# All of w_out for the two full tiles in split single-pass products, its first halves made during the dense stage, and two expert units prefetched later

## The reference

```
proj  = x @ w_in + b_in                      # 1024 -> 7168: xa ga b c v m_a m_b
h     = rglru(conv4(xa))                     # gates, recurrence over positions
mixed = (sigmoid(m_a) * h * gelu(ga) + sigmoid(m_b) * b * conv3(c * v)) @ w_out   # 1024 x 1024
x     = layernorm(ALPHA * x + mixed)
gates = softmax(top4(x @ router_w + router_b))              # of 32 experts
x     = layernorm(ALPHA * x + sum_e gate_e * ((up + 1) * gate * sigmoid(1.702 gate)) @ w_down[e])
```

## Time and profile before

| | us |
|---|---|
| runs shown, median (lowest, highest) | 1194.64 (1194.02, 1195.10) |
| profiled execution, its own time | 1193.83 |
| its span, from first to last record | 1192.1 |
| PE busy in the span | 1144.1 (96%) |
| DVE busy | 520.6 (44%) |
| ACT busy | 260.0 (22%) |
| DMA: bytes moved, mean rate | 443.78 MB, 372 GB/s |
| granted TensorE clock, mean | 0.994 of full speed |

### The profile page before, as it was taken

The page is one execution under the profiler, slowest core; times in us unless marked ns, Lnnn a source line. Parts: engine busy times, 40 slices in busy tenths (PEclk is TensorE's granted clock), DMA queues, the critical chain, the costliest instruction groups (busy, mean ns, idle before and its releaser), DMA issues.

```text
span 1192.1 us, 13955 instructions
## 1 busy us (share of the span) xinstructions
PE 1144.1 (96%) x5682; PEld 555.9 (47%) x5682; DVE 520.6 (44%) x989; ACT 260.0 (22%) x405; POOL 3.3 (0%) x13
## 2 busy tenths in 40 slices
PE   9999999999999999999999989999999999999994
PEld 8999999663333333333333323333333333333331
DVE  6788788883333333333333332333333333333336
ACT  4655655411111111111111111111111111111112
POOL 1000000000000000000000000000000000000000
PEclk9999999999999999999999999999999999999998
DMA  9866964768999999999999999999999999999994
GB/s 231 263 207 174 265 194 130 290 280 347 384 428 426 427 428 428 428 426 428 428 427 428 427 428 427 428 426 428 429 427 427 426 429 428 426 429 427 427 425 161
DMA packets 93853, 443.78 MB, mean 372 GB/s; under 512 B 7912, under 2 KB 65400, under 8 KB 68062
## 3 DMA queue, kind: packets, MB, share of 16 engines
q1 hardware_dynamic: 93614, 442.41, 92.1%
q10 hardware_dynamic: 176, 0.48, 0.1%
HBM read 441.34 MB, written 1.53 MB: 372 GB/s over the span
## 4 chain that ended last, share of the span: by engine, by line
PE 65%; DMA 24%; DVE 7%; ACT 2%; issue 2%; SPq 0%; DVEq 0%; POOL 0%; ACTq 0%; POOLq 0%
PE PS L949 25%; DMA ring<-in_w_gu 19%; PE PS L990 13%; PE PS L737 8%; PE PS L854 6%; DMA ring<-in_w_down 4%; PE PS L876 3%; PE PS L758 2%; DVE w_lo L1096 2%; PE PS L862 1%; DVE tiles L1139 1%; PE PS L869 1%; PE PS L913 1%; PE PS L768 1%; PE PS L1030 1%
## 5 line engine op out<-in xcount | busy, mean ns | idle before, releaser
L949 PE MATMUL PS<-ring,mid 128*64 128x512 f32 x1920 | 422.0, 593 | 20.4 <-DMA ring<-in_w_gu 19.8
L949 PEld LDWEIGHTS PS<-ring,mid 128*64 128x64 f32 x1920 | 135.8, 137 | 299.8 <-issue 258.5
L990 PE MATMUL PS<-ring,mid 128*64 128x512 f32 x952 | 211.3, 595 | 0.0
L1421 DVE TENSOR_SCALAR PS<-PS 128x512 f32<-128x512 f32 x30 | 21.0, 700 | 353.1 <-PE PS L949 353.1
L737 PE MATMUL PS<-x_hi,w_hi 128*128 128x320 f32 x448 | 140.5, 314 | 1.9 <-ACT tiles L555 1.1
L737 PE MATMUL PS<-x_lo,w_hi 128*128 128x320 f32 x448 | 138.4, 309 | 0.0
L737 PE MATMUL PS<-x_hi,w_lo 128*128 128x320 f32 x448 | 138.4, 309 | 0.0
L1403 DVE TENSOR_TENSOR ys<-PS,ys 64x512 fp32r<-64x512 f32 x64 | 44.1, 689 | 193.9 <-ACT ys L642 185.6
L990 PEld LDWEIGHTS PS<-ring,mid 128*64 128x64 f32 x952 | 65.6, 137 | 129.5 <-issue 129.5
L1139 DVE SCALAR_TENSOR_TENSOR x_tok<-PS,gate,x_tok 128x1024 f32<-128x1024 f32 (+1 forms) x93 | 115.2, 1276 | 20.9 <-PE PS L876 20.9
L633 ACT ACTIVATE mid<-PS 128x512 f32<-128x512 f32 x30 | 17.9, 597 | 418.8 <-DVE PS L1421 418.8
(11 more groups left out here) (243 smaller groups left out, 756.2 us busy)
## 6 DMA issues: line engine op xcount, KB each, us to landing
ring<-in_w_gu SPq DMA_DIRECT2D x124, 2048.0 KB, 41.7
ring<-in_w_down SPq DMA_DIRECT2D x59, 2048.0 KB, 40.3
raw<-in_w_in SPq DMA_DIRECT2D x56, 512.0 KB, 5.8
ring<-in_w_down SPq DMA_DIRECT2D x9, 1024.0 KB, 11.9
ring<-in_w_gu SPq DMA_DIRECT2D x8, 1024.0 KB, 7.5
ring<-in_w_out SPq DMA_DIRECT2D x4, 1024.0 KB, 5.0
x_tok<-in_x_prompt SPq DMA_DIRECT2D x2, 512.0 KB, 4.9
x_tok<-in_w_down SPq DMA_DIRECT2D x1, 1024.0 KB, 12.3
```

The costliest lines, as they stand in the source:

```text
L949: last = mm(PS[64 * a:64 * a + 64, b, :], xgT[:, 2 * (u % 2) + j, u // 2, :], w[2 * j + b][:, a * HALF:(a + 1) * HALF], start=False, stop= ...
L990: last = mm(PS[64 * a:64 * a + 64, XB, :], hT[:, j, u, :], w[j][:, a * HALF:(a + 1) * HALF], start=(u == 0 and j == 0), stop=(u == 1 and j ...
L1421: dve.tensor_scalar(gm, gm, LIMIT, None, ALU.min).then_inc(gm_ok, 1)
```

## The change

`HALVED` falls from (0, 1, 2, 4, 10) to (0, 1, 4): units 2 and 10 are whole. `EARLY = {4: 2, 5: 3, 6: 0, 7: 1}` names which chunk of w_out is split in which chunk of the dense stage. `out_hi` now lies in slot 10, `out_lo` in slot 1, so that both exist before the dense stage ends; `out2_hi`, `out2_lo`, `mix2_hi` and `mix2_lo` (slots 9, 8, 7 and in place of `mixT`) hold the parts for chunks 4 to 7. `project` serves tile 2 alone.

```
@@ SP, dense loads
-                    if k < 6:
-                        load_half(k // 2, k % 2).then_inc(unit_in[k // 2], 16)
-                    elif k < KC:
-                        load_out(k - 6)
-                    else:
-                        load_half(10, k - KC).then_inc(unit_in[10], 16)
+                    if k < 4:
+                        load_half(k // 2, k % 2).then_inc(unit_in[k // 2], 16)
+                    elif k == 4:
+                        load_out(1)
+                    elif k == 6:
                         sp.wait_ge(bias_ok, 1)
+                        load_out(0)
@@ SP, after proj_done NP
             load_unit(6)
-            load_unit(9)
+            load_unit(3)
+            sp.wait_ge(first_read, 1)
+            sp.wait_ge(outlo_ok, 2 * HALF_K)
+            load_half(4, 1).then_inc(unit_in[4], 16)
+            load_half(FREED, 0).then_inc(freed_in, 16)
             sp.wait_ge(block_ok, KC + 1)
             load_unit(5)
             sp.wait_ge(first_free, 1)
-            load_unit(3)
-            load_half(4, 1).then_inc(unit_in[4], 16)
-            load_half(FREED, 0).then_inc(freed_in, 16)
+            load_unit(2)
+            load_unit(10)
             sp.wait_ge(wout_done, 5)
             load_unit(8)
+            load_unit(9)
@@ ACT, in the dense loop, before the wait for proj_done
+                if j == 3 and c in EARLY:
+                    k = EARLY[c]
+                    act.wait_ge(wout_in[k // 2], 16)
+                    act.activation(out_hi[:, k, :], out_rows(k // 2)[:, k % 2, :], ACT.Copy).then_inc(outhi_ok, 1)
+                if j == 4 and c == KC - 1:
+                    act.wait_ge(wcur_ok, KC)
+                    act.wait_ge(block_ok, HALF_K + 1)
+                    for t in range(2):
+                        act.activation(mix_s[:, t, 0], mix_of(t), ACT.Copy).then_inc(mixhi_ok, 1)
@@ ACT, after it (the copies of L582 and L586 are gone)
+            for k in range(HALF_K):
+                act.wait_ge(wout_in[2 + k // 2], 16)
+                act.activation(out2_hi[:, k, :], out_rows(2 + k // 2)[:, k % 2, :], ACT.Copy).then_inc(out2hi_ok, 1)
+            act.wait_ge(block_ok, KC + 1)
             for t in range(2):
+                act.activation(mix2_hi[:, t], mix_of(t, slice(HALF_K, KC)), ACT.Copy).then_inc(mix2hi_ok, 1)
@@ PE
             for k in range(KC - 1):
                 pe.wait_ge(block_ok, k + 2)
                 pe.wait_ge(wout_in[k // 2], 16)
-                for a in range(2):
-                    last = project(2, a, [k])
+                last = project(k)
                 if k == HALF_K - 1:
                     last.then_inc(first_read, 1)
...
+            last.then_inc(second_read, 1)
+            pe.wait_ge(outlo_ok, 2 * HALF_K)
             pe.wait_ge(mixlo_ok, 2)
             for a in range(2):
+                project_split(0, a, False)
+            pe.wait_ge(block_ok, KC + 1)
+            project(KC - 1).then_inc(wout_done, 1)
+            for a in range(2):
+                last = project_split(1, a, False)
             last.then_inc(first_free, 1)
-            for a in range(2):
-                project(1, a, range(HALF_K, KC)).then_inc(wout_done, 1)
+            pe.wait_ge(mix2lo_ok, 2)
+            for t in range(2):
+                for a in range(2):
+                    project_split(t, a, True).then_inc(wout_done, 1)
@@ DVE, dense loop: out_low(c, h) is half a chunk, 128 x 512, with then_inc(outlo_ok, 1)
+                if c in EARLY:
+                    out_low(c, 0)
+                if c == KC - 1:
+                    out_low(c, 1)
+                    for t in range(2):
+                        dve.wait_ge(mixhi_ok, t + 1)
+                        dve.tensor_tensor(mix_s[:, t, 1], mix_of(t), mix_s[:, t, 0].bitcast(F32), ALU.subtract)\
+                           .then_inc(mixlo_ok, 1)
                 taken(7)
...
+                if c in EARLY and c < KC - 1:
+                    out_low(c, 1)
                 ahead(10)
@@ DVE, after it (L1259 to L1267 are gone)
+            dve.wait_ge(second_read, 1)
+            out2_low(0)
+            out2_low(1)
             for t in range(2):
+                dve.wait_ge(mix2hi_ok, t + 1)
+                dve.tensor_tensor(mix2_lo[:, HALF_K:KC, t * P:(t + 1) * P], mix_of(t, slice(HALF_K, KC)),
+                                  mix2_hi[:, t].bitcast(F32), ALU.subtract).then_inc(mix2lo_ok, 1)
+            out2_low(2)
+            dve.wait_ge(wout_done, 1)
+            out2_low(3)
```

More of the change, by code:

```diff
@@ L24 @@
 SLOTS, UNITS = 11, 6
-HALVED = (0, 1, 2, 4, 10)
+HALVED = (0, 1, 4)
 SLOT_OF = (2, 0, 1, 4, 3, 5, 6, 7, 8, 9, 10)
@@ L64 @@
 LG_BANK = {2: 4, 0: 5, 1: 0}
+EARLY = {4: 2, 5: 3, 6: 0, 7: 1}
 PREV, LIST = LOOP - 1, 24
@@ L261, in hybrid_layer @@
         wout_done, shifted = sem("wout_done"), sem("shifted")
+        second_read, mix2hi_ok, mix2lo_ok = sem("second_read"), sem("mix2hi_ok"), sem("mix2lo_ok")
+        out2hi_ok, out2lo_ok = sem("out2hi_ok"), sem("out2lo_ok")
         mixhi_ok, mixlo_ok, outhi_ok, outlo_ok = (sem(n) for n in ("mixhi_ok", "mixlo_ok", "outhi_ok", "outlo_ok"))
@@ L294, in hybrid_layer @@
         HALF_K = KC // 2
[L295 to L300, removed]
+        out_hi = place("out_hi", [P, HALF_K, D], 10 * slot, F32R)
+        out_lo = place("out_lo", [P, HALF_K, D], slot, F32R)
+        out2_hi = place("out2_hi", [P, HALF_K, D], 9 * slot, F32R)
+        out2_lo = place("out2_lo", [P, HALF_K, D], 8 * slot, F32R)
         def half_of(n, h):
@@ L314, in hybrid_layer, with mix_of @@
         mix_s = place("mix_s", [P, 2, 2, HALF_K, P], X1, F32R)
-        def mix_of(t):
-            return mixT[:, 0:HALF_K, t * P:(t + 1) * P]
+        mix2_hi = place("mix2_hi", [P, 2, HALF_K, P], 7 * slot + 8 * D, F32R)
+        mix2_lo = place("mix2_lo", [P, KC, T], MID, F32R)
+        def mix_of(t, ks=slice(0, HALF_K)):
+            return mixT[:, ks, t * P:(t + 1) * P]
         ln2g, ln2b = half_of(UNITS * NE, 0)[:, 0:D], half_of(UNITS * NE, 0)[:, D:2 * D]
@@ L410, in _ @@
                     k = (q - 7) // 4
-                    if k == 6:
-                        sp.wait_ge(bias_ok, 1)
-                    if k < 6:
-                        load_half(k // 2, k % 2).then_inc(unit_in[k // 2], 16)
-                    elif k < KC:
-                        load_out(k - 6)
-                    else:
-                        load_half(10, k - KC).then_inc(unit_in[10], 16)
+                    if k < 4:
[3 more added lines that the diff above has]
+                    elif k == 6:
+                        sp.wait_ge(bias_ok, 1)
+                        load_out(0)
             sp.dma_start(rw[:, :, :], router_w[0].rearrange("(k p) e -> p k e", p=P)).then_inc(misc_in, 16)
@@ L576, in turned @@
                 act.activation(xT[:, :, t0:t0 + n], src, ACT.Copy).then_inc(x1T_ok, 1)
-            act.wait_ge(wcur_ok, KC)
-            act.wait_ge(block_ok, HALF_K + 1)
+            for k in range(HALF_K):
+                act.wait_ge(wout_in[2 + k // 2], 16)
+                act.activation(out2_hi[:, k, :], out_rows(2 + k // 2)[:, k % 2, :], ACT.Copy).then_inc(out2hi_ok, 1)
+            act.wait_ge(block_ok, KC + 1)
             for t in range(2):
[L582 to L586, removed]
+                act.activation(mix2_hi[:, t], mix_of(t, slice(HALF_K, KC)), ACT.Copy).then_inc(mix2hi_ok, 1)
             act.wait_ge(wout_done, 1)
@@ L751, in _, with project, project_split @@
             pe.wait_ge(proj_taken, KC + 7 * KC)
[L752 to L759, removed]
+            def project(k):
+                t0, n = TILES[2]
+                for a in range(2):
+                    last = mm(PS[64 * a:64 * a + n, 4, :], mixT[:, k, t0:t0 + n],
+                              out_rows(k // 2)[:, k % 2, a * HALF:(a + 1) * HALF], start=(k == 0), stop=(k == KC - 1))
                 return last
-            def project_split(t, a):
+            def project_split(t, a, second):
                 cols = slice(a * HALF, (a + 1) * HALF)
                 for k in range(HALF_K):
[L766 to L769, removed]
+                    if second:
+                        pe.wait_ge(out2lo_ok, k + 1)
+                        x_hi2, x_lo2 = mix2_hi[:, t, k, :], mix2_lo[:, HALF_K + k, t * P:(t + 1) * P]
+                        w_hi2, w_lo2 = out2_hi[:, k, cols], out2_lo[:, k, cols]
+                    else:
+                        x_hi2, x_lo2 = mix_s[:, t, 0, k, :], mix_s[:, t, 1, k, :]
+                        w_hi2, w_lo2 = out_hi[:, k, cols], out_lo[:, k, cols]
+                    for n, (x, w) in enumerate(((x_hi2, w_hi2), (x_lo2, w_hi2), (x_hi2, w_lo2))):
+                        last = mm(PS[:, 2 * t + a, :], x, w, start=(not second and k == 0 and n == 0),
+                                  stop=(second and k == HALF_K - 1 and n == 2))
                 return last
@@ L774, in _ @@
                 pe.wait_ge(wout_in[k // 2], 16)
-                for a in range(2):
```

(32 more changed lines are left out.)

## The result

The changed kernel takes 1200.6 us, median of 6 runs (1199.32 to 1201.2); the kernel before took 1194.33 (6 runs, 1193.2 to 1195.1). The ratio is 1.005, 95% interval 1.004 to 1.006: slower by 0.5%. The forecast of 1195.5 us with its range from 1193.3 to 1198.8 was wrong. The profiled execution is the fastest of the six (1199.32 us) and has a span of 1197.6 us.

What follows compares the result with a forecast made beforehand. The weight stream was taken as the bound, its end set by the first slot release. Dense stage 0, start of experts +0.9 and ring 0 gave +0.9 us: 1195.5 us against the median, range 1193.3 to 1198.8.

Steps and rivals of the forecast that it cites:

- The frame: Weight stream sets the end: time of PE's first slot release plus a constant, if the units that fit are loaded.
- The dense stage at 0: Dense stage: added ACT copies and DVE halves for early parts fit idle time, costing 0; uncovered, 4 x 1 us.
- w_out on PE and DVE's wait at +0.9: w_out to start of experts: PE done 3.1 us earlier, but DVE waits for tile 0; tile 1's second half +0.9 us.
- The 0.2 us for the change of tiling: w_out on PE: some 0.2 us allowed for changing the tiling, between 64 and 128 columns.
- the 0.5 us of the last product: w_out on PE: tile 0's last product is out about 0.5 us after its load, at 246.4.
- The ring at 0: Weight stream: late units still fill the ring 5 us before the first release; cost 0, uncovered up to 9.8 us.
- rival 3: Weight stream: late units miss the first release; one unit +5.8 us (1200.4), both +10.7 (1205.3); chance 7%.
- rival 1: PE's gap before second logits: clock falls, up to 1.65 us, with the 0.9 up to +2.5, say 1196.8; chance 25%.
- program order puts them behind tile 1's first half: w_out on PE: tile 0's chunks 4 to 7 close after tile 1's first half; the argument against rival 2.
- rival 2: Start of experts: DVE does not hold tile 1 up, PE's earlier end comes through; at most -2.9, 1191.7; chance 10%.

Runs made afterwards that it cites:

- e1: Changed kernel with 2 products of 128x512 ahead of tile 0's transposes and 9 ahead of the second logits, filling PE's gap: 1195.04 us, ratio 1.0005.
- e3: Kernel before, with ACT held up by five copies of 128x320 ahead of its copy of tile 0's transposes, so PE idles: 1202.85 us, ratio 1.0073.
- e4: Changed kernel with tile 0's second half moved on PE directly behind tile 2's last chunk, ahead of tile 1: 1191.76 us, ratio to kernel before 0.9978.
- e5: Changed kernel, gap left open, with 12 products of 128x512 directly behind the wait for ACT's copy, ahead of the second logits: 1198.84 us, ratio 1.0039.
- e2: Changed kernel with 2 products of 128x512 ahead of tile 0's transposes, 5 ahead of second logits: 6 runs 1194.10 to 1194.95, 4 runs 1199.34 to 1202.43 us.

## Why the prediction was wrong

**The frame was right.** The end moves with the first expert product: from it to the end of the span are 921.2 us before, 921.8 after and in e1, 921.4 in e3, 921.9 in e4, 921.7 in e5. The 0.2 to 0.7 us that the kernels with the change take longer there were not followed up.

**The dense stage at 0** was right: 156.0 to 156.1 us for six chunks in the changed kernel, e1, e2, e4 and e5, against 156.25. What the span won ahead of it, 1.4 us at c = 1, is of this one execution: e1, e2, e4 and e5, with the same instructions there, have that mark at 64.97, 64.12, 64.80 and 64.49, and before it stood at 64.77. The profile of the changed kernel therefore shows a loss of 5.5 us of span, where the medians show 6.3.

**w_out on PE and DVE's wait at +0.9** measured +0.68. Tile 0's first sum stood 25.26 us behind the last gate products (forecast 25.4), tile 1's second half 8.97 us behind that (9.05). The 0.2 us for the change of tiling and the 0.5 us of the last product come from no row; the chain after joins its pieces at 232.54 and 233.55 without a break. e1 shows this part of the change with the clock held: a ratio of 1.0005, 0.6 us, and not told apart from nothing.

**The ring at 0** (rival 3) was right: unit 7 goes out at 266.67, the queue is empty from 276 us (a DMA share of 0.01 from 276 to 280), the first released load follows at 279.46, and e1 pays nothing for the late units.

**What failed is the price of rival 1, which the sum left out and the range cut off.** The mechanism stood there: a gap of 2.8 us (2.56 measured), then a fall of the clock. But the step "A fall costs up to what it cost there, 1.65 us" took the price from the one fall of the trace, where the twelve gather products of 128x512 followed and the low stretch was over after (1.00 - 0.88) x 14 / 0.50 = 3.4 us. Here logits, transposes and mask products followed, the clock stayed down for 13.7 us, and the way to the first expert product grew by 5.75 us. The prediction's own words could have warned: it saw "5 us of short PE products" behind the gap (8.1 us from the second logits to the gather before), and at half the clock each of them costs its own length again, more than 1.65 us. e5 shows that the work behind the gap makes the difference between 3.4 and 13.7 us. Put in afterwards, 0.7 + 5.75 = 6.4 us on the 1194.33 us of the kernel before give 1200.8, against 1200.6 measured; this is bookkeeping and no second forecast, since 5.75 comes from the run that it explains.

The chance of 25% was too low as well. That "weight loads and short products stand close ahead of it" did not prevent the fall: all 6 runs of the changed kernel took over 1199 us, and e3 makes the fall with a gap of 2.12 us in the other kernel. The Trainium skill ("TensorE: Matmul & The Clock Gate", "Why this matters for your kernels") names the direction, and the trace agrees: 2.56 us idle, then a clock of 0.50. Its figure is gaps of over about 3 us, and there the measurement decides: 2.56 and 2.12 us were enough here.

**The other side** of the same order was missed as a chance. The prediction saw that "program order puts them behind tile 1's first half" and took it as given; e4 is that order turned round. It meets the condition that rival 2 names, tile 0 closed by 243 us (its first sum is at 242.65), and the time from the last gate products to tile 1's second half falls by 33.55 - 30.77 = 2.8 us, close to the 2.9 that rival 2 gives.

## What to carry to other kernels

When a change shortens one engine's work and another engine then holds it up, price the idle time that this makes on TensorE, not only the wait: about two and a half microseconds of it cost nearly six here. Take that price from a fall with the same kind of work behind it: here the clock took 3.4 us to come back behind products of 128x512, and 10 to 14 behind logits and transposes. And when partial sums are closed in turns, close first the one whose consumer is next in line; it removed both the wait and the gap.

## What the runs showed of the hardware

- A gap of 2.12 to 2.56 us was followed by a granted clock of 0.50 in each of the three profiles that have one (after, e3, e5). The clock fell 0.6 to 1.5 us behind the end of the gap, with PE at work again. Gaps of 1.19 and 0.30 us in the profiles of e2 and e1 were not followed by a fall.
- With 1.2 us idle the outcome was open: 6 of 10 runs near 1194.5 us, 4 from 1199.3 to 1202.4, of which none was profiled.
- At half clock 16 logit products took 3.62 us for 1.97. The gather took 4.13 us for 2.94; it got the full clock back on its way.
- With logits, transposes and mask products behind the gap the low stretch lasted 13.7 us (after) and 10.2 us (e3); with twelve products of 128x512 right behind it, 3.4 us (e5, and the gap at 707 us before).
- The same logits and transposes without a gap kept the full clock: 1.00 from 250 to 275 us before and in e4.
